# Six instead of four token tiles gathered in an expert layer, routing in two passes, row fetches spread by one timetable

## What is computed

```python
qh = (xb @ peer_wq).reshape(PEER_BLOCK, PEER_HEADS, 2, PEER_HALF)
s = jnp.einsum('thpc,hpkc->thpk', qh, peer_keys).astype(jnp.float32)
sv, si = lax.top_k(s, PEER_TOPK)
cand = sv[:, :, 0, :, None] + sv[:, :, 1, None, :]
...
gate = jax.nn.softmax(cv, axis=-1).reshape(PEER_BLOCK, -1)
u = jnp.take(peer_u, eid, axis=0)
vv = jnp.take(peer_v, eid, axis=0)
a = jax.nn.gelu(jnp.einsum('td,ted->te', xb, u).astype(jnp.float32), approximate=False) * gate
return jnp.einsum('te,ted->td', a.astype(xb.dtype), vv)
```

## Time and profile before

| | us |
|---|---|
| median of 3 runs (3922.56 to 3937.77) | 3932.12 |
| the profiled execution's own time | 3930.59 |
| its span, first to last instruction | 3928.8 |

### The profile page before, as it was taken

One profiled execution on the slowest core, in us unless ns is written; L12 is line 12 of the kernel. 1 busy time (PEld: TensorE's weight loads), 2 busy tenths in 40 slices (PEclk: granted clock), 3 DMA queues, 4 the chain that ended last, 5 costly groups with the idle time before them and its releaser, 6 DMA issues. The chain is left out here.

```text
span 3928.8 us, 46712 instructions
## 1 busy us (share of the span) xinstructions
PE 3275.3 (83%) x17014; PEld 2498.8 (64%) x17014; DVE 2523.9 (64%) x5636; ACT 1089.0 (28%) x2099; POOL 1704.9 (43%) x1327
## 2 busy tenths in 40 slices
PE   6999478999985877296677999988999998999897
PEld 5889357778873766295455666666666665666554
DVE  3000267777742899895998777777777777776333
ACT  3111133433422111084112222222222222222221
POOL 0000000000000233295777777777777777676553
PEclk9999689999996888698888999999999999999999
DMA  3222301111113010078999999999999999999887
GB/s 134 85 91 76 123 32 47 53 36 46 37 36 114 22 32 11 3 205 263 351 352 356 411 392 392 384 407 392 391 393 379 411 388 397 383 391 363 327 337 266
DMA packets 303458, 914.67 MB, mean 233 GB/s; under 512 B 30358, under 2 KB 114478, under 8 KB 285596
## 3 DMA queue, kind: packets, MB, share of 16 engines
q0 software_dynamic: 167088, 608.95, 39.8%
q1 hardware_dynamic: 133804, 302.61, 21.8%
q10 hardware_dynamic: 2368, 0.53, 0.1%
HBM read 848.84 MB, written 64.32 MB: 232 GB/s over the span
## 5 line engine op out<-in xcount | busy, mean ns | idle before, releaser
L1025 POOL DMA_INDIRECT ex_row_u<-in_u_rows,eid_u x576 | 730.4, 1268 | 352.1 <-DVE ex_dots L1100 190.8
L1031 POOL DMA_INDIRECT ex_row_v<-in_v_rows,eid_v x576 | 719.0, 1248 | 289.0 <-issue 154.2
L1100 DVE CUSTOM_DVE_ANT_0 ex_row_u<-ex_row_u,ex_h2n 128x1024 f32<-128x1024 f32 x576 | 701.0, 1224 | 21.9 <-DMA ex_row_u<-in_u_rows,eid_u 21.9
L1211 PE MATMUL ex_psum_v<-ex_a_hi,ex_v_hi 128*128 128x512 f32 x1024 | 427.9, 418 | 157.0 <-DVE ex_y L1153 142.5
L1153 DVE TENSOR_TENSOR ex_y<-ex_y,ex_psum_v 128x512 f32<-128x512 f32 x504 | 339.5, 683 | 213.5 <-PE ex_psum_v L1211 180.1
L1195 PE MATMUL ex_psum_u<-h2d_hi,ex_u_hi 128*128 128x512 f32 x1024 | 411.2, 402 | 31.5 <-DMA ex_spike<-in_consts 25.3
L665 POOL TENSOR_TENSOR rt_w_lo<-rt_w_raw,rt_w_hi 128x1024 fp32r<-128x1024 f32 x16 | 37.6, 2365 | 869.7 <-ACT rt_w_hi L431 869.7
L1211 PE MATMUL ex_psum_v<-ex_a_lo,ex_v_hi 128*128 128x512 f32 x1024 | 414.8, 405 | 0.0
L1179 PE MATMUL ex_psum_g<-ex_row_v,ex_mask 128*32 128x512 f32 x2304 | 324.5, 688 | 108.3 <-ACT ex_mask L1064 89.9
L1211 PE MATMUL ex_psum_v<-ex_a_hi,ex_v_lo 128*128 128x512 f32 x1024 | 414.4, 405 | 0.0
L1195 PE MATMUL ex_psum_u<-h2d_lo,ex_u_hi 128*128 128x512 f32 x1024 | 403.2, 394 | 0.0
(11 more groups left out here) (298 smaller groups left out, 5700.1 us busy)
## 6 DMA issues: line engine op xcount, KB each, us to landing
ex_u_raw<-in_u SPq DMA_DIRECT2D x64, 1024.0 KB
ex_v_raw<-in_v SPq DMA_DIRECT2D x64, 1024.0 KB
gates<-gt_out SPq DMA_DIRECT2D x8, 4096.0 KB, 15.9
ex_gate<-gates SPq DMA_DIRECT2D x64, 512.0 KB
mx_pj<-proj SPq DMA_DIRECT2D x9, 1796.0 KB, 7.4
proj<-pj_out SPq DMA_DIRECT2D x63, 225.0 KB, 2.0
pj_w_raw<-in_w_in SPq DMA_DIRECT2D x6, 1800.0 KB, 7.7
ex_row_u<-in_u_rows,eid_u POOLq DMA_INDIRECT x576
```

The source lines that it names most:

```text
L1025: nc.gpsimd.indirect_dma_start(row_u[:, r % UR, :], None, u_rows, bass.IndirectOffsetOnAxis(eid_u[:, r:r + 1], 0)).then_inc(u_row[r % UR], 16)
L1031: nc.gpsimd.indirect_dma_start(row_v[:, r % VR, :], None, v_rows, bass.IndirectOffsetOnAxis(eid_v[:, V_TOK[r]:V_TOK[r] + 1], 0)).then_inc( ...
L1100: nc.vector.tensor_tensor_reduce(row_u[:, r % UR, :], row_u[:, r % UR, :], h2n[:, n % 2, :], 1.0, 0.0, ALU.mult, ALU.add, dots[:, n % 2, r ...
L1211: last = nc.tensor.matmul(psum_v[:, i % VB, :], a[:, j, d * P:(d + 1) * P], b[:, (s - 1) % 2, j, :], start=(m == 0), stop=(m == 3 * JG - 1))
```

## The change

- **Tiles.** Six prompt tiles (768 tokens) are gathered; two prompt tiles and the sample tokens (320) are dense. There are 768 `u` and 768 `v` fetches. In the dense stage matmuls and element-wise instructions have 320 columns instead of 512, and there are 5 gate blocks instead of 8.
- **Routing in two passes.** `route` runs once for the six gathered tiles (tag ra) and once for the three tiles of the dense ones (tag rb), which loads the query weights again. The loops over heads are written out.
- **One timetable.** It now covers the 8 heads of the second routing, 10 half blocks of the gate stage and 64 + 4 dense steps. Targets are 26 fetches a head, 16 a half block and (1536 - 368) / 64 = 18.25 a dense step. It also gives GpSimd's fetches their places. As the buffers of the rings let it, it puts 185 fetches into the second routing (19, then 24 a head five times, 30 and 16, 16 `v`), 176 into the gate stage (32 into its first half block), and 1175 into the rest. 152 `u` fetches go first, so nearly all of those in routing are `u`: 169 dot products and 4 quads stand there. The last 152 fetches are `v`: at most 16 a step from dense step 56 on, the last of them in steps 64 and 65, of which 64 has only the product by `v` and 65 no dense work. Rings are UR = VR = 8.
- **Gate stage.** The multiplication by the gate moves from GpSimd to ScalarE (four 128x128 instructions per four tokens), and all one-hot rows are VectorE's.
- **First experts.** The load and split of `u[0]` beside the gate stage (`FirstExperts`) is gone; it is done at the start of the dense stage.
- **Constants of mixing** are loaded by GpSimd's queue during the projection (`MixConstants`).

```diff
-GT = 4
-DBASE = GT * P
-DTOK = SEQ - DBASE
-GTOK = TOK - DTOK
+GT = 6
+GTOK = GT * P
+DTOK = TOK - GTOK
...
+            def meanwhile(h, place):
+                if G and h < PH:
+                    G.on_dve(dve, G.table.ROUTE + h, place)
...
+                    meanwhile(h, 2 * p)
...
+                meanwhile(h, 4)
...
+                meanwhile(h, 6)
...
+            def meanwhile(h, place):
+                if G:
+                    G.on_pool(pool, G.table.ROUTE + h, place)
+            low(0)
+            for h in range(PH):
+
+                if h:
+                    look_up(h - 1, 0, pick, "stairs")
+                meanwhile(h, 0)
+                low(2 * h + 1)
+                meanwhile(h, 1)
+                if h:
+                    look_up(h - 1, 1, look, "hot")
+                meanwhile(h, 2)
+                if h + 1 < PH:
+                    low(2 * h + 2)
+                meanwhile(h, 3)
+                meanwhile(h, 4)
+            look_up(PH - 1, 0, pick, "stairs")
...
+            each_key = iota[:, :].unsqueeze(1).to_broadcast([P, 4, NK])
+            for i in range(UNITS):
+                if i >= OH // 4:
+                    dve.wait_ge(multiplied, i + 1 - OH // 4)
+                nc.vector.tensor_tensor(hot_j[:, slot(i), :], each_key, spread(sel_j, i), ALU.is_equal)
+                nc.vector.tensor_tensor(one_i[:, slot(i), :], each_key, spread(sel_i, i),
+                                        ALU.is_equal).then_inc(compared, 1)
+                if i % 2:
+                    G.on_dve(dve, G.table.GATES + i // HALF, i % HALF // 2)
...
+            for half in range(2 * NB):
+                for place in range(2):
+                    G.on_pool(pool, G.table.GATES + half, place)
...
+            def gate(i):
+                act.wait_ge(compared, i + 1)
+                for r in range(4):
+                    at = hot_j[:, 4 * i % OH + r, :]
+                    last = nc.scalar.activation(at, at, ACT.Copy, scale=sel_g[:, 4 * i + r:4 * i + r + 1])
+                last.then_inc(gated, 1)
...
+UR, VR = 8, 8
...
+IN_ROUTE, IN_GATES = 26, 16
...
+    AHEAD = P + 24
+    DUE = 7
+    LANDING = 5
...
+        route=dict(dve=(0.1, 0.25, 0.4, 0.55, 0.7, 0.85, 0.97), act=(0.3, 0.8), pe=(0.35, 0.85),
+                   pool=(0.0, 0.2, 0.4, 0.6, 0.8), sp=(0.95,)),
...
+        left = (len(fetches) - IN_ROUTE * PH - IN_GATES * 2 * NB) / GROUPS
+        self.rates = [IN_ROUTE] * PH + [IN_GATES] * (2 * NB) + [left] * (GROUPS + self.TAIL)
...
+        dot_at, quad_at, ready, free, fetched, quad = {}, {}, {}, {-1: 0.0}, 0.0, 0.0
+        for f in fetches:
+            kind, r = f
+            n, k = r // P, r // 4
+            slot_free = dot_at.get(r - UR, 0.0) if kind == "u" else quad_at.get((r - VR) // 4, 0.0)
+            fetched = self.put("pool", self.rows, max(fetched, slot_free, self.due(f, 0)), f)
...
+                quad = quad_at[k] = self.put("pe", self.quads, max(here, ready[n], free[n - 1], quad), k)
...
+    def on_dve(self, dve, s, place):
+        nc = self.nc
+        for r in self.table.dots.get((s, place), ()):
+            n = r // P
...
+            row = self.row_u[:, r % UR, :]
+            nc.vector.tensor_tensor_reduce(row, row, self.h2n[:, n % 2, :], 1.0, 0.0, ALU.mult, ALU.add,
+                                           self.dots[:, n % 2, r % P:r % P + 1]).then_inc(self.dotted, 1)
...
+                for s in range(ALL):
+                    for place in range(2):
+                        G.on_pool(pool, at(s), place)
...
-                                    last = nc.tensor.matmul(psum_u[:, i % 2, :], a[:, j, k, :], b[:, k, :],
+                                    last = nc.tensor.matmul(psum_u[:, i % 2, 0:DTOK], a[:, j, k, :], b[:, k, :],
...
+    def load(self, pool, I):
+        pool.dma_start(self.cs[:, :], I["consts"][:, 0:C_MIX]).then_inc(self.loaded, 16)
...
+            route(nc, "ra", (g_hi, g_lo), GTOK, I["wq"], I["keys"], ident_d, places_d, starts_d,
+                  eid=(eid_u, eid_v, gate_n))
...
+            route(nc, "rb", hd, DTOK, I["wq"], I["keys"], ident_d, places_d, starts_d, sel=(sel_i, sel_j, sel_g),
+                  gathered=G)
+            gate_matrices(nc, sel_i, sel_j, sel_g, iota_d, gates, G)
```

More of the change, by code:

```diff
@@ L293, in _ @@
                 sp.wait_ge(s, 16 * (NT // RING) * blocks)
+        @block.gpsimd
+        def _(pool):
+            mc.load(pool, I)
         @block.scalar
@@ L474, in _ @@
         def _(pe):
-            def body(h, first):
+            for h in range(PH):
                 for p in range(2):
@@ L566, in body @@
                     dve.wait_ge(score_out, hp + 1)
-                    if not first and p == 1:
+                    if h and p == 1:
                         first_keys_of(h - 1)
-                    for t in range(NT):
+                    for t in range(n_tiles):
                         last = nc.vector.max(top_v[:, p, t, 0:8], score[:, p, t, :])
@@ L593, in step @@
                         dve.wait_ge(pick.sem, pick.at(h, name))
-                if not first:
+                if h:
                     gates_of(h - 1)
@@ L787, in _ @@
         @block.gpsimd
         def _(pool):
-            def body(b, first):
-                for q in range(Q):
-                    s = (4 * q) % OH
-                    if not (first and q < OH // 4):
-                        pool.wait_ge(multiplied, b * Q + q + 1 - OH // 4)
-                    pool.wait_ge(compared_j, b * Q + q + 1)
-                    nc.gpsimd.tensor_tensor(gate_j[:, s:s + 4, :], hot_j[:, s:s + 4, :], spread(sel_g, b, q),
-                                            ALU.mult).then_inc(gated, 1)
@@ L817, in _ @@
-            body(0, True)
-            with pe.Fori(1, NB) as b:
-                body(b, False)
+            for i in range(UNITS):
+                pe.wait_ge(gated, i + 1)
+                if i >= 4:
+                    pe.wait_ge(copied, i - 3)
+                for r in range(4):
+                    s = 4 * i % OH + r
+                    last = nc.tensor.matmul(psum[:, i % 4, r, :], one_i[:, s, :], hot_j[:, s, :], start=True, stop=True)
+                last.then_inc(multiplied, 1)
+                if i % 4 == 3:
+                    G.on_pe(pe, G.table.GATES + i // HALF, i % HALF // 4)
@@ new lines, in _ @@
+            gate(0)
+            gate(1)
+            for i in range(UNITS):
+                b, q = i // Q, i % Q
+                if i + 2 < UNITS:
+                    gate(i + 2)
+                if q == 0 and b >= 2:
+                    act.wait_ge(stored[b % 2], b // 2 * 16)
+                act.wait_ge(multiplied, i + 1)
+                nc.scalar.activation(out[b % 2][:, :, 4 * q:4 * q + 4],
+                                     psum[:, i % 4, :, :].rearrange("p t j -> p j t"), ACT.Copy).then_inc(copied, 1)
+                if i % 4 == 3:
+                    G.on_act(act, G.table.GATES + i // HALF, i % HALF // 4)
```

906 lines of the change are left out of this document (399 added, 507 removed).

## The result

The changed kernel takes 4587.2 us (median of 4 runs, 4583.6 to 4601.1), the kernel before 3934.9 us beside it (4 runs). The ratio is 1.167 (95% interval 1.163 to 1.171): 652 us slower, where 349 were forecast. The direction was right; the time lies above the top of the range, 4430.

A forecast was written before the change was run, and what follows sets the result against it. The prediction took full DMA engines, with TensorE close, to bound the dense stage's middle, and VectorE the routing. Its terms, -25 + 261 + 173 + 8 - 68 = +349 us, gave 3930.6 + 349 = 4280 us, range 4110 to 4430.

The forecast's parts named there:

- Constants of mixing, -25: Before mixing: loading its constants under the projection, where GpSimd is idle, saves 25 us (bounds -29 to -20).
- First pass, 302: Routing of the six gathered tiles: eight heads of 31.5 us plus 50 for start and end, 302 us.
- Nearly all of VectorE's part grows with the tiles: Routing: a head of n tiles takes 4 + 41.2 n / 9 us, 31.5 for six and 17.7 for three.
- Second pass, 381: Routing of the other three tiles: 8 x 17.7 us, 169 dot products and 45 for start and end, 381 us.
- 169 x 1.15: Second routing pass: 169 dot products on VectorE at 1.15 us each, added to the heads' time.
- Gate stage, 310: Gate stage: 300 us by DMA time, 310 with some gaps, instead of 137, so +173 us.
- 5 x 14.9 + 176 x 1.28: Gate stage's DMA time: five blocks at 14.9 us and 176 fetches at 1.28 us, 300 us.
- Dense stage, 2027: Dense stage: 56 steps of 30.5 us, 8 of 32 and 63 at the end, 2027 for 2095, so -68 us.
- What doesn't shrink is DMA: Dense step: 12.0 MB still move, 29.2 us at 411 GB/s or 30.6 at 393; 30.5 taken.
- Rival A: DMA has more in hand; GpSimd's issue bounds dense steps at 23.2, say 24 us: 3790 us in all, chance 0.04.
- Rival C: TensorE becomes the dense stage's bound at its lower clock: 33 us a step, 4440 us in all, chance 0.13.
- The check by bytes: Whole kernel without a stage model: 960 MB after the first pass at 411 GB/s give 3967 us even without DMA pauses.

The follow-up runs named there:

- e1_lows_early: Changed kernel with GpSimd making each low part of a query weight ahead of the look_up it stood behind: 4485.9 us, ratio to the kernel before 1.140.
- e3_no_fetch_in_routing: e1_lows_early with no fetch in the second routing pass, those fetches left to later stages: 4809.0 us.
- f2_fetches_singly: e1_lows_early with GpSimd's fetches allowed at 16 places of a dense step and 8 of a gate half block, for 2 each: 4337.7 us, ratio 1.104.
- two small edits: Each on e1_lows_early: fetches at more places (f2_fetches_singly, 4337.7 us), or ScalarE's third dense place at 0.45 for 0.42, making masks earlier (4350.6 us).
- g5f_five_tiles_singly: f2_fetches_singly with five gathered tiles for six: 4264.0 us, ratio 1.085.

## Why the prediction was wrong, point by point

- **Constants of mixing, -25.** Alone, 25 us between the medians and 23 by the ratio. By the start of the routing it is 18 us in the changed kernel and 19 alone (1230 for 1249), under my bound of 20; the rest came in the routing, whose reason is open. "They are now loaded under the projection" was taken as free: the gap shrank by 26.4 us, and the projection grew by 9 to 11.
- **First pass, 302.** The head's 31.5 us was right to the tenth once VectorE sets the pace (e1_lows_early). The step that failed is "Nearly all of VectorE's part grows with the tiles", taken as the whole head: I scaled the engine that was full before and did not follow GpSimd's list, in which the change had put each low part behind a `look_up`. The program's order showed that, and e1_lows_early prices it at 90 us. The 50 us for the pass's start and end were 15 too many (35 measured), which hid a part of it.
- **Second pass, 381.** 18.3 us for my 17.7 (e3_no_fetch_in_routing). The term "169 x 1.15" (194 us) failed: dot products and their surroundings cost 267 us. Of the 73 us more, 37 are dot products that take 1.37 us apiece, and 36 are VectorE's idle time. Most of what a steady head has over 45.9 us is 6.2 us in one dot product, in which VectorE waits for GpSimd's tensor instructions; 20 us of the idle time are waits for `u` rows in the last heads, where `v` rows have begun (periods up to 59 us); the rest of it was not taken apart. "Nothing hides the dot products there" stood. The 45 us for start and end were 23 too many (22 measured), so the error of the pass is smaller than that of the term. "GpSimd needs 24 x 1.27 us" left out 0.3 us between issues and GpSimd's own tensor work: it was busy for 322 of 442 us, not hidden.
- **Gate stage, 310.** The sum by DMA time (300 us) came near for a wrong reason, since half the bytes changed nothing. The step that failed is to take DMA's time, 5 x 14.9 + 176 x 1.28, as the stage's. 25 of the 34 us of error are the places of the fetches. What the rest is was not isolated; in f2_fetches_singly TensorE still waits there for masks (147 us), and e3_no_fetch_in_routing, with no quad in the stage, is 59 us shorter there.
- **Dense stage, 2027.** "What doesn't shrink is DMA" is right as a floor and wrong as the step: one of two small edits had to bring the stage to it (2046 and 2032). My sentence that rows of four or five dot products stand before the last two additions saw the row there, and missed the one before the second product with the gates, with the mask behind it in ScalarE's list. Price: 129 to 143 us by the two edits, for an error of 131.
- **Rival A** said GpSimd's issue would allow steps of 23.2 us. It was further off than my 0.04 says: GpSimd's 1.61 us a fetch makes 29.5 for 18.3 fetches, so no step under 26 was to be had with these.
- **Rival C** was nearest, 33 us a step for 32.5 measured, and its "rows of dot products hold it up" is the mechanism. It read the clock rightly, 0.82 for 0.84. Its title was wrong: TensorE was busy for only 66% of the stretch, and in f2_fetches_singly for 73% at a clock of 0.86, with DMA full. It was held up and did not set the pace. That the size fits is partly luck, as the price of the rows had been taken as 5 x 1.15 us.
- **The check by bytes** (3967 us even if DMA never pauses) stood as a bound for the sign. With both edits the same 1536 fetches take 4332 us. Fewer fetches alone give little (g5f_five_tiles_singly, 1280 fetches, 4264 us); with some 254 of them moved into the dense stage it is 4031. So where they stand weighs more here than how many there are.

## What to carry to other kernels

When an engine's list is rewritten, ask of every producer in it what it now stands behind; a 0.9 us mask behind an instruction that waits for a row of fetches cost 130 us, and a low part behind a look-up 90 us, while every engine's total stayed small. A stage scaled from the busiest engine gives a floor, not a time; halving one resource (bytes, instructions) in a run of its own tells whether it alone is the limit; where two lie together, as DMA and GpSimd here, halving one shows little. A load put "under" another stage competes with that stage's own loads. And before trading a full resource for idle ones, count what the new load costs on its issuer too.
